# Prompt stick-breaking: running log-sums in one stream of scaled chunks, with the accumulation on GpSimd

## The reference, cut to what matters

```
z = einsum('bqhd,bkhd->bhqk', q, k) / sqrt(64) + bias[head]
mask = k_pos < q_pos
log_1m = where(mask, log_sigmoid(-z), 0)
rest = cumsum(log_1m, axis=keys, reverse=True) - log_1m
a = where(mask, exp(log_sigmoid(z) + rest), 0)
o = einsum('bhqk,bkhd->bqhd', a, v)
```

## Time and profile before

| | us |
|---|---|
| median of three runs (lowest, highest) | 3425.09 (3420.98, 3427.0) |
| the profiled execution, whole | 3432.7 |
| its span, first to last instruction | 3431.2 |
| busy over the span: PE, DVE, ACT, POOL | 2973.1, 1714.4, 1516.2, 572.9 |

### The profile page before, as it was taken

How to read it: one execution, slowest core, us unless ns; L and a number is a source line. 1 busy time by engine, 2 the same in 40 slices (tenths; PEclk the granted TensorE clock), 3 DMA queues, 4 the chain that set the end, 5 groups by cost and what they waited for, 6 DMA issues and landing times. The chain is left out here.

```text
span 3431.2 us, 53450 instructions
## 1 busy us (share of the span) xinstructions
PE 2973.1 (87%) x17230; PEld 2082.8 (61%) x17230; DVE 1714.4 (50%) x3114; ACT 1516.2 (44%) x3146; POOL 572.9 (17%) x1137
## 2 busy tenths in 40 slices
PE   8999789996898989897999966888878876499998
PEld 5888668885444444443878854455545543388887
DVE  2000042222898989897666533333333333666663
ACT  3212232221887878786655532233323322433342
POOL 0000012121312222221000003343334410000000
PEclk9999899998999999999999978989989988699999
DMA  5444444445001010002333229999999977522321
GB/s 182 154 168 163 162 152 164 147 171 192 25 1 38 1 38 1 13 1 62 98 87 75 52 67 331 386 386 384 373 380 386 379 263 305 174 93 98 117 92 39
DMA packets 315997, 548.80 MB, mean 160 GB/s; under 512 B 65474, under 2 KB 159138, under 8 KB 312676
## 3 DMA queue, kind: packets, MB, share of 16 engines
q1 hardware_dynamic: 273252, 344.53, 30.0%
q0 software_dynamic: 42496, 201.23, 15.9%
HBM read 485.95 MB, written 126.68 MB: 179 GB/s over the span
## 5 line engine op out<-in xcount | busy, mean ns | idle before, releaser
L1239 POOL DMA_DIRECT2D sbs_v_ring<-in_cache_v_sb x512 | 276.1, 539 | 901.0 <-issue 898.5
L416 PE MATMUL proj_ps_G<-proj_w_hi,proj_xT_hi 128*128 128x512 f32 x1024 | 401.9, 392 | 3.1 <-DVE proj_xT_lo L288 3.1
L420 PE MATMUL proj_ps_G<-proj_w_hi,proj_xT_lo 128*128 128x512 f32 x1024 | 399.0, 390 | 0.0
L418 PE MATMUL proj_ps_G<-proj_w_lo,proj_xT_hi 128*128 128x512 f32 x1024 | 399.0, 390 | 0.0
L1325 DVE COPY sbs_kT<-sbs_ps_T 128x512 f32<-128x512 f32 x256 | 176.1, 688 | 415.2 <-PE sbs_ps_T L1486 415.1
L1486 PE MATMUL sbs_ps_T<-sbs_ident,sbs_k_ring 128*128 128x128 f32 x2048 | 297.7, 308 | 98.6 <-DMA sbs_k_ring<-in_cache_k_sb 85.1
L1486 PEld LDWEIGHTS sbs_ps_T<-sbs_ident,sbs_k_ring 128*128 128x128 f32 x2048 | 267.2, 160 | 139.4 <-DMA sbs_k_ring<-in_cache_k_sb 93.2
L360 ACT ACTIVATE proj_out<-proj_ps_G,proj_stat 128x512 f32<-128x512 f32 (+1 forms) x136 | 93.4, 688 | 567.1 <-PE proj_ps_G L420 562.4
L288 DVE TENSOR_TENSOR proj_xT_lo<-proj_ps_T,proj_xT_hi 128x512 fp32r<-128x512 f32 (+1 forms) x68 | 42.3, 662 | 510.5 <-ACT proj_xT_hi L350 510.5
L721 PE MATMUL sbp_Z<-sbp_S,sbp_suffix 128*128 128x512 f32 (+3 forms) x576 | 258.2, 531 | 0.0
L585 DVE TENSOR_TENSOR sbp_sp_lo<-sbp_sp,sbp_sp_hi 128x512 fp32r<-128x512 f32 (+3 forms) x320 | 200.2, 639 | 49.2 <-POOL sbp_sp_hi L545 28.8
(11 more groups left out here) (266 smaller groups left out, 5751.3 us busy)
## 6 DMA issues: line engine op xcount, KB each, us to landing
sbs_v_ring<-in_cache_v_sb POOLq DMA_DIRECT2D x512, 256.0 KB, 6.0
sbs_k_ring<-in_cache_k_sb SPq DMA_DIRECT2D x512, 256.0 KB, 9.6
out_k_win_s<-in_cache_k_win POOLq DMA_DIRECT2D x16, 2044.0 KB, 9.2
out_v_win_s<-in_cache_v_win POOLq DMA_DIRECT2D x16, 2044.0 KB, 8.6
proj_out<-in_w_in SPq DMA_DIRECT2D x32, 512.0 KB, 5.5
proj_x_in<-in_x_prompt SPq DMA_DIRECT2D x32, 512.0 KB, 3.7
dls_k_in<-in_cache_k_win SPq DMA_DIRECT2D x16, 1024.0 KB, 10.5
dls_v_in<-in_cache_v_win SPq DMA_DIRECT2D x16, 1024.0 KB, 13.9
```

The lines of the kernel that those rows point to most:

```text
L416: nc.tensor.matmul(ps_G[0:n, g, :], xT_hi[:, slot, k, 0:n], w_hi[:, k, cols], start=(k == 0), stop=False)
L418: nc.tensor.matmul(ps_G[0:n, g, :], xT_hi[:, slot, k, 0:n], w_lo[:, k, cols], start=False, stop=False)
L420: mm = nc.tensor.matmul(ps_G[0:n, g, :], xT_lo[:, slot, k, 0:n], w_hi[:, k, cols], start=False, stop=(k == KC - 1))
L1239: eng.dma_start(ring[:, q % RING, i, :], cache[bass.ds(page, 1), :, :].rearrange("a s c -> (a s) c")) \
```

## The change

The carried sum moves from the exponent to a factor. In the new form a step subtracts from z only what lies in its own tile. Its product with v, one chunk for both heads, goes to a PSUM bank of its own, `L`, and not to an accumulator. PE also adds up the column sums of sp over the steps of a Q, for both heads in one bank, `total` (`totals`: four one-pass matmuls with a matrix of ones, none in the last step of a Q). ACT takes exp(total) into `E` (`left`), DVE multiplies L by E into `LE` (`scale`, 512 columns for both heads together), and POOL adds LE to `acc` in SBUF (`add`, 512 columns, both inputs in SBUF). `cut`, S and its float32 matmul are gone, and so is `oT`.

Besides:
- bias enters z by one more 64-row matmul for each head, so `exp`, `ln` and `weights` are one instruction for both heads, 1024 columns in full steps; `softplus` becomes min(max(z, 30), ln(1 + exp z)).
- both high parts are made by POOL, in two casts; both low parts stay on DVE. The two triangular masks of a step are one instruction.
- the four pairs are one stream of 160 steps, g. Fills (four of 1024 columns for each pair) and the output transposes ("turn", one for each Q) are entries of the same list, `SLOTS`, and take one of the three slots of Z as a step does. An entry of index k+2 is prepared while entry k is finished. A pair's fills stand before steps 8, 16, 24 and 32 of the pair before; turns stand before steps 4, 8, 16 and 28 of a pair.
- most tiles in SBUF go from four buffers to two for each head. `left(g)` waits until `scale(g-2)` has been done, and `weigh(g)` until `scale(g-1)` has.
- PE waits for v only before the first `sums`, and q and k come in halves. DVE makes constants at the start (some 16 small instructions).

```diff
...
-    NI = 2 * NP
-    FILLS = 2 * NQ
-    ZB = 6
...
+    G = NP * PAIRS
+    FILLS = 4
+    ZS = 3
+    LINEAR = 30.0
...
+    FILL_AT = {}
+    for p in range(PAIRS):
+        for f in range(FILLS):
+            FILL_AT.setdefault(0 if p == 0 else NP * (p - 1) + 8 * (f + 1), []).append(("fill", p, f))
+    TURN_AT = {closing(p, Q) + 5: ("turn", p, Q) for p in range(PAIRS) for Q in range(NQ)}
+    SLOTS = []
+    for g in range(G):
+        SLOTS += FILL_AT.get(g, [])
+        if g in TURN_AT:
+            SLOTS.append(TURN_AT[g])
+        SLOTS.append(("step", g, None))
+    K = len(SLOTS)
+    SLOTS.append(("turn", PAIRS - 1, NQ - 1))
+    SLOT = {x: n % ZS for n, x in enumerate(SLOTS)}
+    TAKEN_FROM = {x: SLOTS[n - ZS] for n, x in enumerate(SLOTS) if n >= ZS}
...
+        Z = m.ps("Z", [P, ZS, 2, 512])
+        total = m.ps("total", [P, 512])
+        L = m.ps("L", [P, 512])
...
+            def high(g):
+                c, b = first_col(g), g % 2
+                if diagonal(g):
+                    pool.wait_ge(sp_done, 2 * g + 2)
+                    blk = sp_[:, b, :, c:c + P]
                     nc.gpsimd.affine_select(out=blk, in_=blk, compare_op=ALU.is_gt, fill=0.0, base=0,
...
+                                            pattern=[[0, 2], [1, P]], channel_multiplier=-1).then_inc(sp_masked, 1)
+                    pool.wait_ge(sp_masked, diags_to(g))
+                for h in range(2):
+                    if not diagonal(g):
+                        pool.wait_ge(sp_done, 2 * g + h + 1)
+                    if g >= 2:
+                        wait_split_read(pool, g - 2)
+                    nc.gpsimd.tensor_copy(sp_hi[:, b, h, c:512], sp_[:, b, h, c:512]).then_inc(hi_done, 1)
+            def cover(g):
+                c = first_col(g)
+                pool.wait_ge(a_done, g + 1)
+                blk = a[:, g % 2, :, c:c + P]
                 nc.gpsimd.affine_select(out=blk, in_=blk, compare_op=ALU.is_gt, fill=0.0, base=0,
...
+                                        pattern=[[0, 2], [1, P]], channel_multiplier=-1).then_inc(a_masked, 1)
+            def add(g):
+                p, Q, j, s = step(g)
+                if s > 0:
+                    c0 = first_col(g - 1)
+                    pool.wait_ge(L_read, g + 1)
+                    if scaled_to(g) > 1:
+                        pool.wait_ge(acc_done, scaled_to(g) - 1)
+                    nc.gpsimd.tensor_tensor(acc[:, Q % 2, c0:512], acc[:, Q % 2, c0:512], LE[:, g % 2, c0:512],
+                                            ALU.add).then_inc(acc_done, 1)
+            for k in range(-2, K):
+                kind, g, _ = entry(k)
+                if kind == "step" and diagonal(g):
+                    cover(g)
+                new, x, _ = entry(k + 2)
+                if new == "step":
+                    high(x)
+                if kind == "step" and g > 0:
+                    add(g - 1)
+            add(G - 1)
...
+            for p in range(PAIRS):
+                nc.vector.tensor_scalar(bias_row[:, p, :], zeros[:, :], bias_at[:, p:p + 1], None, ALU.add).then_inc(set_up, 1)
...
+            def softplus(g, h):
+                c, b = first_col(g), g % 2
+                if h == 0:
+                    dve.wait_ge(ln_done, g + 1)
+                if g >= 2:
+                    dve.wait_ge(lo_done, 2 * g + h - 3)
+                nc.vector.scalar_tensor_tensor(out=sp_[:, b, h, c:512], in0=Z[:, z(g), h, c:512], scalar=LINEAR,
+                                               in1=el[:, b, h, c:512], op0=ALU.max, op1=ALU.min).then_inc(sp_done, 1)
+            def low(g, h):
+                c, b = first_col(g), g % 2
+                dve.wait_ge(hi_done, 2 * g + h + 1)
+                nc.vector.tensor_tensor(sp_lo[:, b, h, c:512], sp_[:, b, h, c:512],
+                                        sp_hi[:, b, h, c:512].bitcast(F32), ALU.subtract).then_inc(lo_done, 1)
+            def scale(g):
+                p, Q, j, s = step(g)
+                c, c0 = first_col(g), 512 if s == 0 else first_col(g - 1)
+                dve.wait_ge(av_done, g + 1)
+                if s == 0 and NQ * p + Q >= 2:
+                    dve.wait_ge(o_turned, NQ * p + Q - 1)
                 if c < c0:
...
+                    dve.wait_ge(E_done, scaled_to(g))
+                    if g >= 2 and scaled_to(g - 2) > 0:
+                        dve.wait_ge(acc_done, scaled_to(g - 2))
+                    op = nc.vector.tensor_tensor(LE[:, g % 2, c0:512], L[:, c0:512], E[:, g % 2, c0:512], ALU.mult)
+                op.then_inc(L_read, 1)
+            for k in range(-2, K):
+                (kind, g, _), (new, x, y) = entry(k), entry(k + 2)
+                weighed = g - 1 if kind == "step" and g > 0 else None
+                if weighed is not None:
+                    scale(weighed)
+                if new == "fill":
+                    fill(x, y)
+                if new == "step":
+                    softplus(x, 0)
+                    softplus(x, 1)
+                if new == "step":
+                    low(x, 0)
+                    low(x, 1)
+            scale(G - 1)
...
+            def left(g):
+                c0 = first_col(g - 1)
+                act.wait_ge(total_done, totals_to(g - 1))
+                if g >= 2:
+                    act.wait_ge(L_read, g - 1)
+                nc.scalar.activation(E[:, g % 2, c0:512], total[:, c0:512], ACT.Exp).then_inc(E_done, 1)
+            for k in range(-2, K):
...
+                if new == "turn":
+                    put_out(x, y)
+                if new == "step":
+                    exp(x)
+                if kind == "step":
+                    weights(g)
+                if new == "step":
+                    ln(x)
+                if kind == "step" and g + 1 < G and step(g + 1)[3] > 0:
+                    left(g + 1)
...
+                for h in range(2):
+                    r = slice(h * DH, (h + 1) * DH)
+                    nc.tensor.matmul(Z[:, z(g), h, c:512], lift_r[r, :], bias_row[r, p, c:512], start=True, stop=False,
+                                     skip_group_check=True)
...
+            def sums(g):
+                c, b = first_col(g), g % 2
+                for h in range(2):
+                    pe.wait_ge(hi_done, 2 * g + h + 1)
+                    nc.tensor.matmul(Z[:, z(g), h, c:512], suf_r[:, :], sp_hi[:, b, h, c:512], start=False,
                                      stop=False, skip_group_check=True)
...
+                for h in range(2):
+                    pe.wait_ge(lo_done, 2 * g + h + 1)
+                    nc.tensor.matmul(Z[:, z(g), h, c:512], suf_r[:, :], sp_lo[:, b, h, c:512], start=False,
+                                          stop=True, skip_group_check=True).then_inc(sum_done, 1)
+            def totals(g):
+                c, b, (p, Q, j, s) = first_col(g), g % 2, step(g)
+                if j == 0:
+                    return
+                if scaled_to(g) > 0:
+                    pe.wait_ge(E_done, scaled_to(g))
+                for n, part in enumerate((sp_hi, sp_lo)):
+                    for h in range(2):
+                        mm = nc.tensor.matmul(total[:, c:512], all_r[:, h, :], part[:, b, h, c:512],
+                                              start=(s == 0 and n == 0 and h == 0), stop=(j == 1 and n == 1 and h == 1),
+                                              skip_group_check=True)
+                mm.then_inc(total_done, 1)
+            def weigh(g):
+                c, (p, Q, j, s) = first_col(g), step(g)
+                if diagonal(g):
+                    pe.wait_ge(a_masked, diags_to(g))
                 else:
...
+                    pe.wait_ge(a_done, g + 1)
+                if g > 0:
+                    pe.wait_ge(L_read, g)
                 for h in range(2):
...
+                    mm = nc.tensor.matmul(L[h * DH:(h + 1) * DH, c:512], v_all[:, j, p * P + h * DH:p * P + (h + 1) * DH],
+                                          a[:, g % 2, h, c:512], start=True, stop=True, skip_group_check=True)
                 mm.then_inc(av_done, 1)
...
+            pe.wait_ge(consts, 48)
+            for k in range(-2, K):
+                (kind, g, _), (new, x, y) = entry(k), entry(k + 2)
+                if new == "fill":
+                    fill(x, y)
+                if new == "turn":
+                    turn_out(x, y)
+                if new == "step":
+                    if x == 0:
+                        pe.wait_ge(set_up, 12 + PAIRS)
+                    score(x)
+                if kind == "step":
+                    if g == 0:
+                        pe.wait_ge(v_loaded, 16)
+                    sums(g)
+                    totals(g)
+                    if g > 0:
+                        weigh(g - 1)
...
```

More of the change, by code:

```diff
@@ L547, in cover @@
[L547 to L561 removed]
+            nc.gpsimd.memset(zeros[:, :], 0.0).then_inc(zeroed, 1)
@@ L580, in low @@
[L580 to L594 removed]
+            nc.vector.tensor_copy(suf_r[:, :], suffix[:, 0, :]).then_inc(set_up, 1)
```

(2 more changed lines are left out.)

380 lines of the change are left out of this document (155 added, 225 removed).

## The result

The changed kernel takes 3444.11 us (median of five, 3437.36 to 3445.37) beside 3427.0 us (3420.98 to 3429.93) for the kernel before, a ratio of 1.0048 with a 95% interval of 1.0034 to 1.0062. Timed once more beside it (experiment 11) it came out at 1.0033 (1.0022 to 1.0044). So it is slower by 0.3 to 0.5%, 9 to 17 us. The forecast was slower, by 48 us. In the profiled executions the span went from 3431.2 to 3435.9 us, 4.7 us more. That the medians are 17 us apart and these two only 5 is scatter of the executions: the profiled one of the kernel before lies 5.7 us above the median of its runs (3432.7 against 3427.0), and that of the changed kernel is the shortest of its five (3437.4 against a median of 3444.1).

What follows compares the result with a forecast made beforehand. PE was taken to set the pace of a full step at 4.75 us. Full steps +12, diagonals -8, gaps +53, start -10 and end +1 made +48 us on 3432.7, less 7.6: 3473 us, range 3360 to 3520.

Steps and rivals of the forecast that it cites:

- part 3: DVE and POOL in full steps: `low` of head 1 is held by `add`; 4.87 us against 4.75, 96 steps, +12 us.
- part 5: Fills and turns in the lookahead: 5.7 us a double, 3.3 a single, 84 us less 31, +53 us.
- 21 gaps: Time lost at fills and turns: 6 doubles and 15 singles, 34 + 50 = 84 us.
- change of pair gone: Drain between pairs, 10.2 us more than a step, three times, no longer paid: 31 us less.
- Part 1: PE in a full step: 4.07 us after the change; PE alone would gain 0.68 us in each.
- R: Time `add` reads SBUF ahead of `low` of head 1 in a full step: taken as 1.0 us (0.43 to 1.29).
- T: Length of DVE's loop in a full step: 4.87 us (4.30 to 5.16).
- Part 4: Diagonal steps: the same loop at widths 128 to 512, 16 groups, -8 us (-24 to +10).
- Part 6: The ends: first `sums` at about 855.5 in place of 865.67, -10 us; +1 at the end.
- A: Full step: reads hold each other up less, or `low` goes ahead of `add`; PE paces; 3363 us, chance 0.20.
- B: Fills and turns: holding as forecast, but the lookahead absorbs the gaps (20 us for 21); 3409 us, chance 0.18.
- C: PE idles in every gap and comes back at the lower clock level, +25 us; 3498 us, chance 0.12.

Runs made afterwards that it cites:

- experiment 11: The changed kernel unedited, timed once more beside the kernel before: 3438.0 us beside 3429.5, ratio 1.0033.
- experiment 7: The changed kernel with turns taking no place in the lookahead, ScalarE copying the sum to the output tile instead of transposes: 3404.2 us, ratio 0.9934.
- Experiments 8 and 9: The kernel before, with one of three pairs of `score` matmuls left out (ratio 0.9986), and with `cut` left out (0.9919).
- experiments 1 to 3: The changed kernel with `add` on VectorE (ratio 0.9835), on GpSimd ahead of its casts (0.9877), or cut to one column (0.974).
- experiment 3: The changed kernel with GpSimd's `add` cut to the first column of its range, all waits kept: 3345.1 us, ratio 0.974.
- experiment 12: The changed kernel with GpSimd's `add` replaced by a copy, one SBUF input in place of two: 3372.9 us, ratio 0.9836.
- experiment 2: The changed kernel with `add` still on GpSimd but issued ahead of the two casts of its step: 3388.9 us, ratio 0.9877.
- experiment 4: The changed kernel with four buffers for E in place of two, so `left` waits for an older `scale`: 3430.1 us, ratio 0.9997.
- experiment 5: The changed kernel with fills before steps 12, 20, 24 and 32, so none stands beside a turn: 3434.5 us, ratio 1.0019.

## Why the prediction was right or wrong

The sign was right, the size was not: +48 us forecast, +9 to +17 measured, +6.5 in the stage of the traces. Two steps failed, each by some 20 us and both the same way: the count of full steps in part 3 and the price of the single gaps in part 5. That the sign survived is in part luck, since what was left of the sum is small beside its terms. For the ledger, experiment 7 gives the length that each step has without a gap (its last pair has neither fills nor turns in the lookahead, only ScalarE's copies); what the changed kernel has above that is charged to the gaps.

| term | forecast, us | traces, us |
|---|---|---|
| full steps | +12 | -7.5 |
| diagonal steps | -8 | -3.0 |
| 21 gaps | +84 | +65.1 |
| change of pair gone | -31 | -33.5 |
| start and end | -9 | -14.7 |
| sum | +48 | +6.4 |

**What bounds the kernel (premise): wrong.** I read 4.75 us off PE's `sums` and took the row of PE behind row of PE as proof that PE paces. Experiments 8 and 9 refute it: the loop was VectorE's at 4.58, but for the last three full steps of a pair. It did no harm to the sum by luck, since the new loop was overrated by the same amount.

**Part 1, PE: nearly.** With the add out of the way PE's pace is 4.20 us, not 4.07. PE didn't become the bound here.

**Part 3, the mechanism: right.** `low` was to be held by `add`, which gets there first. The 2.80 us of the pair show it, and experiments 1 to 3 show it as the pace of the full step: removing, shortening or reordering `add` each take the step to 4.20 or 4.23 us. R was 1.0 and measures 1.09 (experiment 3), 2.7 times the 0.41 of one input (experiment 12), where I had guessed between two and three passes. The rest of the loop was 3.87 and measures 3.62: `scale` to the start of the first `low` is 1.98 us and not 2.06, and a cast holds `low` for 0.42 us, where 0.56 was put in for it. The order at that place was the other one that part 3 names: the second cast is there before `low` of head 0 and isn't stretched (the pair of casts takes 1.21 us), and `low` of head 0 is (1.11). T was 4.87 and is 4.71. Against the true 4.58 that is +0.13 a step, as forecast by +0.12.

The Trainium skill (GPSIMD Engine Reference, section Performance versus the Vector engine) had put R at an estimated 1.1 us; by that rule, the trace agrees (1.09). The rule of the Trainium skill (SBUF - State Buffer, section Who interferes with whom) that the two exclude each other holds too, but "for the whole instruction" is not to be taken as the recorded time: `add` beside `softplus` is recorded at 1.30 us (experiment 2), and holds `low` up for 1.09.

**Part 3, the count of steps: this step failed.** "96 x (4.87 - 4.75)" gives every full step the full width. The sum lags by three steps, so in each of 12 Qs the first three full intervals take 3.81, 4.23 and 4.43 us in place of 4.71: 12 x 1.66 = 20 us less. This is the +12 that became -7.5. The lag has a counterpart in the diagonal steps: the first three intervals of a Q carry the wide `add` of the Q before (+11.1 us against the kernel before), the fourth carries a narrow one (-13.1). With the first interval of the stream, -1.0, these make the -3.0 of **Part 4**, which by the loop's own widths came to -8.

**Part 5, the gaps: chain right, the price of the singles is the second step that failed.** The 6 doubles cost 5.6 us each (33.4 in all) and were forecast at 5.7. The 15 singles cost 2.1 us each (31 in all) and were forecast at 3.3. They are not alike: a turn in the middle of a pair costs 2.7 to 2.8, one at a pair's start 1.6 to 2.5, a fill before the first step of a Q 0.8 to 1.4, one before a full step of the last Q 1.9. Two things are missing in part 5. It took one chain at full width for all: the first interval loses 3.7 us where full steps follow (8.39 in place of 4.71), but 2.2 to 2.3 where narrow ones do. And it had no term for what comes back. Behind the fill before step 32, all at full width, the next two intervals are 4.10 and 3.62, so 1.7 of the 3.7 us return. In the loop in which that fill stands where a step would be finished, GpSimd has no `add`, and the pair of `low` is not held:

```profile
1199.44 1.71 DVE L701 TENSOR_TENSOR sbp_sp_lo<-sbp_sp,sbp_sp_hi 128x512 fp32r<-128x512 f32 x2
```

With 2 us more for the drain at the change of pair, this is the larger failure by a little: +32 in place of +53. Experiment 7 confirms what turns cost in all (34 us against a forecast of 39), experiment 4 the tie to `left`, and the trace of experiment 5 that the singles were overpriced, as two of them are cheaper than one double.

**Part 6: right, a little too small.** The first `softplus` comes 15.1 us earlier relative to the projection, of which PE's first `sums` keeps 11.7 (850.63 against 865.67, 3.4 of the difference from the projection's end); -10 was forecast.

**Rivals.** A (no holding up) is refuted by the 2.80 us. B (20 us for all gaps) had the direction of my error but not its size, 65. C (the clock) has the kind right and the size wrong. The mean clock of the stage is 0.95 in both kernels, but it falls at other places. In the changed kernel the second interval behind a double is 3.68 us where the clock stays up, and up to 4.85 where it falls to the lower of its two levels. By windows, two such intervals (columns of the earlier trace rows):

```profile
926.14:930.99 4.85, 4.74 (x16) 2.35 (x17) 3.65 (x8) 1.97 (x2) 1.21 (x2) 0.65 0.00 0
1313.97:1317.65 3.68, 3.57 (x19) 1.79 (x18) 3.57 (x7) 1.97 (x2) 1.21 (x2) 1.00 0.00 0
```

PE had stood 1.83 us for GpSimd's cast shortly before either. The six such intervals are 4.9 us over six of 3.68 (5.2 in experiment 11). With the turns and fills whose intervals differ between repeats, an estimate of what the lower clock costs is 7 us of the 65 in the first trace and 9 to 10 in that of experiment 11, against the 25 of C.

Four signs were forecast wrongly. PE was to wait for `lo_done` in `sums`; it waits before `totals` for ACT's E (0.24 us at 945.67). Its busy share is 85%, not 80. It was to be idle for 3 us and more around turns and fills; its longest idle time in the stream is 2.6 us, before a turn, for GpSimd's last `add` of the Q. And an `add` of over 1.5 us was to say that R is wrong; it is recorded at 1.59 on average, and R was nearly right, because the record holds a wait of its own (last section).

## What to carry to other kernels

An instruction of GpSimd that reads two tiles in SBUF belongs where VectorE works with at most one tile in SBUF; its order on its own engine was worth 1.6% here, the choice of the engine 0.4% alone and 0.1% beside the other edits, which is within the noise. In a software pipeline every term of a loop has the width of the step it belongs to, not of the step that gives the loop its name: list them by their lag before multiplying by a count. An entry that takes the place of a step also takes that step's work out of the loop: price what comes back with what is lost. To find the engine that paces, measure intervals on each candidate over several steps; two that differ by 4% can both look busy, and taking work from one of them decides.
